# A mixture-of-experts kernel on one core: expert loops of two experts in place of six, and two alternating weight sets in place of three

## The reference, cut to what matters

```
x = x + HierMoE(RMSNorm(x))          # 1088 tokens, width 1024
# each token chooses one of 4 groups, and 2 of the 8 experts in it: 32 experts
y_e = (silu(x_e @ w1[e]) * (x_e @ w3[e])) @ w2[e]     # w1, w3: 1024 x 512; w2: 512 x 1024
out = sum over the token's two experts of gate * y_e
```

## Time and profile before

| | |
|---|---|
| runs, median (lowest to highest) | 1484.2 us (1483.3 to 1484.79) |
| profiled execution, own time | 1485.76 us |
| its span in the trace | 1484.0 us |
| PE busy | 1285.9 us (87%) |
| DVE, ACT, POOL busy | 29%, 22%, 15% |
| bytes moved by DMAs | 275.02 MB, mean 185 GB/s |
| granted clock of the tensor engine, mean | 0.959 |

### The profile page before, as it was taken

The page is one execution under the profiler, slowest core; times in us unless marked ns, Lnnn a source line. Parts: engine busy times, 40 slices in busy tenths (PEclk is TensorE's granted clock), DMA queues, the critical chain, the costliest instruction groups (busy, mean ns, idle before and its releaser), DMA issues.

```text
span 1484.0 us, 37880 instructions
## 1 busy us (share of the span) xinstructions
PE 1285.9 (87%) x16430; PEld 963.0 (65%) x16430; DVE 427.5 (29%) x873; ACT 333.8 (22%) x775; POOL 229.9 (15%) x318
## 2 busy tenths in 40 slices
PE   5899999928999999999998599988877877987886
PEld 2444444415566666666665598878777776887885
DVE  2210010065545645554436521111111111111110
ACT  5200100025444445544432000000000000000001
POOL 3100000012223212212201211111111111111101
PEclk9999999967999999999999799999998999999998
DMA  7021120052022101201218689999997999899961
GB/s 292 15 72 52 41 82 27 27 205 61 9 73 73 70 18 59 73 15 53 86 50 365 237 322 353 354 347 332 367 340 279 361 359 338 293 374 337 346 235 20
DMA packets 39787, 275.02 MB, mean 185 GB/s; under 512 B 9208, under 2 KB 13176, under 8 KB 27340
## 3 DMA queue, kind: packets, MB, share of 16 engines
q1 hardware_dynamic: 32944, 253.78, 45.2%
q0 software_dynamic: 6400, 17.84, 5.0%
q10 hardware_dynamic: 288, 1.05, 0.2%
HBM read 246.32 MB, written 30.48 MB: 187 GB/s over the span
## 4 chain that ended last, share of the span: by engine, by line
PE 77%; issue 12%; DVE 3%; ACT 3%; DMA 2%; POOL 2%; SPq 0%; POOLq 0%; ACTq 0%; DVEq 0%
PE psum L1054 22%; PE psum L791 16%; PE psum L1080 11%; PE psum L906 7%; PE psum L945 4%; PE psum L977 3%; PE psum L1090 2%; PE psum L957 2%; PE psum L745 2%; PE psum L851 2%; PE psum L1045 2%; POOL small L1458 1%; PE psum L760 1%; PE psum L892 1%; DMA xn_rows<-arena 1%
## 5 line engine op out<-in xcount | busy, mean ns | idle before, releaser
L1054 PE MATMUL psum<-arena 128*64 128x80 f32 (+1 forms) x8192 | 330.5, 241 | 47.4 <-issue 47.0
L1054 PEld LDWEIGHTS psum<-arena 128*64 128x64 f32 x8192 | 314.4, 140 | 61.9 <-issue 59.0
L791 PE MATMUL psum<-arena 128*128 128x512 f32 (+1 forms) x576 | 238.1, 574 | 0.0
L1080 PE MATMUL psum<-arena 128*64 128x80 f32 (+1 forms) x4096 | 164.9, 239 | 41.6 <-issue 41.6
L791 PEld LDWEIGHTS psum<-arena 128*128 128x128 f32 x576 | 108.8, 190 | 123.5 <-issue 123.5
L1080 PEld LDWEIGHTS psum<-arena 128*64 128x64 f32 x4096 | 157.2, 139 | 46.2 <-issue 46.2
L906 PE MATMUL psum<-arena 128*128 128x512 f32 x288 | 127.0, 594 | 1.7 <-DVE arena L1909 1.0
L1415 ACT ACTIVATE arena<-psum,slot_gate 96x1024 f32<-96x1024 f32 x32 | 35.5, 1111 | 411.6 <-PE psum L1090 411.6
L745 PE MATMUL psum<-ident,arena 128*128 128x128 f32 (+1 forms) x432 | 65.0, 286 | 46.2 <-DVE arena L1763 18.7
L906 PEld LDWEIGHTS psum<-arena 128*128 128x128 f32 x288 | 53.3, 190 | 63.0 <-issue 61.4
L745 PEld LDWEIGHTS psum<-ident,arena 128*128 128x128 f32 (+1 forms) x432 | 50.7, 139 | 63.7 <-DVE arena L1763 19.9
(11 more groups left out here) (233 smaller groups left out, 1274.1 us busy)
## 6 DMA issues: line engine op xcount, KB each, us to landing
arena<-in_w SPq DMA_DIRECT2D x96, 2048.0 KB, 12.8
arena<-in_x_rows SPq DMA_DIRECT2D x18, 512.0 KB, 5.6
z_rows<-arena SPq DMA_DIRECT2D x9, 980.0 KB, 4.5
arena<-in_w_in SPq DMA_DIRECT2D x1, 7840.0 KB, 23.6
arena<-z_rows SPq DMA_DIRECT2D x9, 768.0 KB, 5.6
arena<-in_w_out SPq DMA_DIRECT2D x1, 4096.0 KB, 16.9
out_y<-arena SPq DMA_DIRECT2D x8, 512.0 KB, 2.6
xn_rows<-arena SPq DMA_DIRECT2D x8, 512.0 KB, 3.0
```

Of the source, the lines that this page charges most:

```text
L791: ins = pe.matmul(o[:, 0:hi - lo], xT[s][:, k, :], w_in[:, k, lo:hi], start=(k == 0), stop=(k == KD - 1))
L1054: ins = pe.matmul(o[c:c + CT, j * EB:j * EB + rows], w[:, k, j * P + c:j * P + c + CT], x[:, k, 0:rows], start=(k == 0), stop=(k == KD - 1))
L1080: ins = pe.matmul(o[c:c + CT, (j % 4) * EB:(j % 4) * EB + rows], w2s[w][:, k, j * P + c:j * P + c + CT], hT[:, k * EB:k * EB + rows], star ...
```

## The change

Three things change.

- **Weight sets.** `SETS` is 2 in place of 3. The arrays of buffers keep three entries, with three semaphores each. Expert 0 uses set 0 and nobody after it does; expert p above 0 uses set 1 + (p - 1) % 2. `load_next` now waits for expert p - 2 to release its buffer (`free = p - 1`). The three early loads are the same as before.
- **Loops of the tensor engine.** Experts 0, 1 and 2 are written out. Experts 3 to 8 are a loop of two experts a round (three rounds, 96 rows), experts 9 to 30 a second loop of two a round (eleven rounds, 80 rows). Expert 31 is written out. The sync engine's loop takes two experts a round as well.
- **Rows of the transposes.** `gather_transposes` and `turn_back` always use 96 rows; the matmuls of the ups and the downs have 96 or 80 as before.

```diff
-SETS = 3
+SETS = 2
...
+        def set_of(p):
+
+            return 0 if p == 0 else 1 + (p - 1) % SETS
...
-            rounds = (NE - SETS) // SETS
+            rounds = (NE - FIRST) // SETS
             with sp_.Fori(0, rounds) as j:
-                for s in range(SETS):
-                    load_next(sp_, SETS * j + SETS + s, s)
-            for p in range(SETS * (rounds + 1), NE):
-                load_next(sp_, p, p % SETS)
+                for i in range(SETS):
+                    load_next(sp_, SETS * j + FIRST + i, set_of(FIRST + i))
+            for p in range(FIRST + SETS * rounds, NE):
+                load_next(sp_, p, set_of(p))
...
-                    ins = pe.transpose(bank(0, 2)[:, k * P:k * P + rows], xe[s][0:rows, k * P:(k + 1) * P],
-                                       ident[0:rows, 0:rows])
+                    ins = pe.transpose(bank(0, 2)[:, k * P:k * P + EB], xe[s][0:EB, k * P:(k + 1) * P],
+                                       ident[0:EB, 0:EB])
...
-                    ins = pe.transpose(bank(6, 2)[0:rows, j * P:(j + 1) * P], yT[:, j, 0:rows], ident[:])
+                    ins = pe.transpose(bank(6, 2)[0:EB, j * P:(j + 1) * P], yT[:, j], ident[:])
...
-            period = 2 * SETS
-
-            def expert(p, j=None):
-
-                b = p if j is None else p + period * j
-                rounds = lambda q, n: 16 * (q // n + 1) + (0 if j is None else 16 * (period // n) * j)
-                w, s, rows = p % SETS, p % 2, rows_of(p)
+            def expert(p, rows, j=None):
+
+                b = p if j is None else p + 2 * j
+                loaded = lambda q: (16 if q == 0 else 16 * ((q - 1) // SETS + 1)) + (0 if j is None else 16 * j)
+                fetched = lambda q: 16 * (q // 2 + 1) + (0 if j is None else 16 * j)
+                w, s, old = set_of(p), p % 2, set_of(p - 1)
...
-            for p in range(1, BIG + 1):
-                expert(p)
-            turns = (NE - BIG - 2) // period
-            with pe.Fori(0, turns) as j:
-                for i in range(period):
-                    expert(BIG + 1 + i, j)
-            for p in range(BIG + 1 + period * turns, NE):
-                expert(p)
+            for p in range(1, FIRST):
+                expert(p, EB)
+            with pe.Fori(0, (BIG + 1 - FIRST) // 2) as j:
+                for i in range(2):
+                    expert(FIRST + i, EB, j)
+            with pe.Fori(0, (NE - 2 - BIG) // 2) as j:
+                for i in range(2):
+                    expert(BIG + 1 + i, EL, j)
+            expert(NE - 1, EL)
```

More of the change, by code:

```diff
@@ L473, in build @@
         r_exp, order_ok, over_ok, over_tab = sem("route_exps"), sem("order_ready"), sem("overflow_ready"), sem("overflow_tables")
-        w1_in, w3_in, w2_in = [[sem(f"expert_{w}_{i}_in") for i in range(SETS)] for w in ("w1", "w3", "w2")]
+        w1_in, w3_in, w2_in = [[sem(f"expert_{w}_{i}_in") for i in range(SETS + 1)] for w in ("w1", "w3", "w2")]
         xe_clear = sem("xe_cleared")
@@ L1037, in _, with gather_transposes @@
             pe.wait_ge(tab_ok, 1)
-            def gather_transposes(s, b, arrived, count, rows):
+            def gather_transposes(s, b, arrived, count):
                 pe.wait_ge(arrived, count)
@@ L1083, in down, with turn_back @@
                 ins.then_inc(yT_full, 1)
-            def turn_back(b, rows):
+            def turn_back(b):
                 pe.wait_ge(yT_ok, b + 1)
@@ L1089, in turn_back @@
                 for j in range(KD):
-                    ins = pe.transpose(bank(6, 2)[0:rows, j * P:(j + 1) * P], yT[:, j, 0:rows], ident[:])
+                    ins = pe.transpose(bank(6, 2)[0:EB, j * P:(j + 1) * P], yT[:, j], ident[:])
                 ins.then_inc(y_full, 1)
-            rows_of = lambda p: EB if p < BIG else EL
-            period = 2 * SETS
-            def expert(p, j=None):
-                b = p if j is None else p + period * j
-                rounds = lambda q, n: 16 * (q // n + 1) + (0 if j is None else 16 * (period // n) * j)
-                w, s, rows = p % SETS, p % 2, rows_of(p)
-                hidden_1(w, s, b, w1_in[w], rounds(p, SETS), rows)
-                down((p - 1) % SETS, b - 1, w2_in[(p - 1) % SETS], rounds(p - 1, SETS), rows_of(p - 1))
+            def expert(p, rows, j=None):
[3 more added lines that the diff above has]
+                w, s, old = set_of(p), p % 2, set_of(p - 1)
+                hidden_1(w, s, b, w1_in[w], loaded(p), rows)
+                down(old, b - 1, w2_in[old], loaded(p - 1), rows)
@@ L1103, in expert @@
                 if p < NE - 1:
[L1104 to L1108, removed]
+                    gather_transposes(1 - s, b + 1, xe_in[1 - s], fetched(p + 1))
+                hidden_3(w, s, b, w3_in[w], loaded(p), rows)
+                turn_back(b - 1)
+            gather_transposes(0, 0, xe_in[0], 16)
@@ L1109, in _ @@
             hidden_1(0, 0, 0, w1_in[0], 16, EB)
-            gather_transposes(1, 1, xe_in[1], 16, EB)
+            gather_transposes(1, 1, xe_in[1], 16)
             hidden_3(0, 0, 0, w3_in[0], 16, EB)
-            for p in range(1, BIG + 1):
-                expert(p)
-            turns = (NE - BIG - 2) // period
-            with pe.Fori(0, turns) as j:
-                for i in range(period):
-                    expert(BIG + 1 + i, j)
-            for p in range(BIG + 1 + period * turns, NE):
-                expert(p)
@@ L1120, in _ @@
-            last = (NE - 1) % SETS
-            down(last, NE - 1, w2_in[last], 16 * ((NE - 1) // SETS + 1), EL)
-            turn_back(NE - 1, EL)
+            for p in range(1, FIRST):
[6 more added lines that the diff above has]
+                    expert(BIG + 1 + i, EL, j)
@@ L1123, in _ @@
+            expert(NE - 1, EL)
+            last = set_of(NE - 1)
+            down(last, NE - 1, w2_in[last], 16 * ((NE - 2) // SETS + 1), EL)
+            turn_back(NE - 1)
             pe.wait_ge(over_ok, 1)
@@ L1134, in _ @@
                     with pe.If(j < total):
-                        gather_transposes(0, NE + j, ov_xe, 16 * j + 16, EB)
+                        gather_transposes(0, NE + j, ov_xe, 16 * j + 16)
                         hidden_1(0, 0, NE + j, ov_w, 48 * j + 48, EB)
@@ L1138, in _ @@
                         down(0, NE + j, ov_w, 48 * j + 48, EB)
-                        turn_back(NE + j, EB)
+                        turn_back(NE + j)
         @block.scalar
```

## The result

The changed kernel takes 1435.0 us (median of four runs, 1430.5 to 1437.1) against 1483.8 us: a ratio of 0.967, 95% interval 0.964 to 0.969, so 49 us less. The profiled execution has a span of 1428.7 us and an own time of 1430.5.

A forecast was written before the change was run, and what follows sets the result against it. TensorE was held by late code fetches; with short loops kept, transfers would bound: 870 + 6 x 20.0 + 23 x 19.5 = 1438.5 us, plus 20.5 us tail, about 1460 us; likeliest case 1440 to 1470, whole range 1443 to 1531.

The forecast's parts named there:

- the projection loop's missing fetches: Projection loop, 144 matmuls, over one block long, fetched no code between 110 and 290 us: two blocks and one ahead kept.
- the idea of a two-block window: A Trainium skill note that TensorE keeps only a two-page code window and should be fully unrolled; the new loops would be refetched.
- the 15.2 us of an unstalled expert: Expert stage: TensorE's time for an 80-row expert, gather transposes included, if the loop's code is kept; 19.6 us before.
- the bound that comes next: Expert stage after the change: weight transfers limit it, 19.5 us an 80-row expert (19.1 to 19.9), 20.0 us a 96-row one.
- a sign of a wrong sum: Stated check: the summed time is wrong if TensorE waits for gathers or its granted clock falls clearly below 0.99 to 1.00.
- The price of two sets: Start of the expert stage: refills wait for expert 1's first up, putting full weight flow at 870 us, at best 857.
- the sum of two ups: Start of refills: they move from 845.1 us to two ups, or 12 us, later.
- Rival A: Expert loops: TensorE keeps fewer than seven blocks, ten more jumps back cost 5.8 us each; 1530 us, chance 0.20.
- Rival B: Second loop only: it asks for a ninth block, so all eight are fetched every round; 1520 us, chance 0.20.
- each block has a fixed place: Second loop: argument that only one block would be lost, not all eight, which the transfers would cover.
- Rival C: Expert stage: slower transfers, 20.4 us an expert, give the gain back; 1480 us, chance 0.08.
- one block missing, covered by the transfers: Second loop: one fetch a round, some 6 us for two experts, 18.2 us an expert, hidden behind slower transfers.

The follow-up runs named there:

- the twins: Loop of six and loops of two, both with two weight sets plus an idle 2 MB transfer behind each refill: 1578.8 us and 1570.6 us.
- the shifted kernel: The changed kernel with spent waits taking the room of fifty instructions ahead of TensorE's expert stage: 1531.9 us, ratio 1.032.

## Why the prediction was right or wrong

**Right:** that TensorE was held by its own code, in blocks of 127 matmuls; that the projection loop's missing fetches count for more than the idea of a two-block window; that seven and eight blocks are kept; the 15.2 us of an unstalled expert (15.4 to 15.6 with 96-row transposes); the place of both loops to a few instructions, the second in eight blocks by 8 of them; that the transfers become the bound. 54 transfers were forecast as some 55. On the Trainium skill's figure (Runtime: NRT & Kernel Launch, Instruction fetch mechanics: 128 KiB in 16 KiB blocks) the runs agree: eight blocks are kept (54 transfers), 12.6 are not (126). The same section's two-page window, in a note that speaks of 32 KiB, doesn't hold for TensorE here.

**The step that failed** is "the bound that comes next". It scaled 349 GB/s by 0.98/0.96 to 356 and took 349/0.96 = 364 as the best possible, hence 19.5 us an expert and never under 19.1. Measured: 380 to 382 GB/s at a share of 0.99 to 1.00, and 6.95 MB / 0.381 = 18.2 us. Over 23 experts that is 30 us. The share isn't a scale on which a starved queue can be read up to a full one; the rate of a stretch that is known to have a backlog was needed, and the twins show that the window of 349 GB/s had none.

In the same step the 96-row experts were called "at the limit now", 20.0 us each, because the share was 0.98. TensorE passed them at 17.96 us each, on weights already loaded, faster than the flow: their weights came in 19.3 us apart (expert 3's by 889.2 us, expert 8's by 985.5), at a share of 0.93, with refills that waited for TensorE. So 20.0 was near for the weights and wrong as a limit.

Two smaller signs came out otherwise than stated. TensorE's waits for weights are 28.0 us over the last 17 experts, 1.6 us each and not 4. And the granted clock fell to 0.93 to 0.96 behind 1107 us, which was named as a sign of a wrong sum; since the DMA share stays at 0.99 to 1.00 there, this is not where the miss lies.

**The price of two sets** was set slightly too high. Refills start at 858.6, as the sum of two ups said. By the packets of queue q1, expert 8's weights were in at 985.5 us, where the forecast had 870 + 120 = 990, and the last weights at 1403.8, where it had 1438.5. Of these 35 us the rate explains 30 (418 us for 23 experts, 18.2 each), the start and the 96-row experts together 4.5. Against it, the tail was longer: 24.9 us from the last weights to the end in place of 20.5. TensorE had waited for the last w1 (until 1392.9) and then had 36 us of its own work, so the last w2 was no longer the thing waited for. 34.7 - 4.4 = 30.3 us is the whole miss of the span, 1459 against 1428.7.

**Rival A** fell: a body of 6.3 blocks is kept. **Rival B** fell for this kernel and came true next to it: its mechanism, a ninth block asked for and then all eight fetched again, is what the shifted kernel shows, and "each block has a fixed place", which I used to dismiss it, is wrong. The changed kernel mostly escapes, with 8 instructions in its eighth block. That is luck as much as forecast: a shift by fifty instructions, nothing in the work, turns the gain into a loss. The forecast's "one block missing, covered by the transfers" was never seen; a round fetched nothing or nine blocks. **Rival C** had the right bound and the wrong rate.

## What to carry to other kernels

When TensorE's idle time is put down to "issue" at even distances, count instructions and look at the queue that carries code. A loop is free of fetches only if all blocks it touches, from its place in memory and not from its length alone, stay within what the engine keeps; here a loop that reached a fraction of a block too far was slower than the long loop it replaced. Count the place, leave a margin of more than a few instructions, and check the number of code transfers in several executions.

A share of busy time doesn't tell the rate: 349 GB/s at 0.96, 371 and 381 at 1.00. Take the rate of the next bound from a stretch where that resource has a backlog, or make one by adding idle transfers.

## What the hardware showed that was not expected

- With some 8 instructions in the eighth block and a jump back, the loop was mostly kept: of the ten jumps in each of four traces with that layout (54, 63, 63 and 81 code transfers), none, one, one and three had nine transfers behind them, the whole loop again. With some 58 instructions in it, seven of ten had.
- A loop that begins, by count, on the last instruction of a block paid two fetches at eight of ten jumps back, 11.4 to 12.8 us instead of 6 to 7.
- Sixteen or fifty instructions that do nothing moved the time by 88 us down and 97 us up.
- In the changed kernel, the six first ups behind waits for weights of 2.5 to 4.2 us took 6.0 to 7.5 us instead of 4.7, at a granted clock of 0.59 to 0.75, between the two levels of 1.2 and 2.4 GHz. The up at 1142.19, behind a wait of 1.17 us, took 4.7 at 1.00.
- With a backlog, weights, gathers and scatters flow at 380 to 388 GB/s; code fetched at the same time costs 1% of that at most, by one run each.
